# A decoder step: q's norm folded into the output norm, k's norm from rounded parts, and another order of the products in a chunk

## The reference

```python
def l2_normalize(x):
    return x * rsqrt(sum(x * x, axis=-1) + EPS)

q = repeat(l2_normalize(q) * 128 ** -0.5, 2)      # 16 heads of q and k, 32 of v
k = repeat(l2_normalize(k), 2)
decay = where(incl, exp(where(incl, gc_i - gc_j, 0)), 0)
a_mat = where(strict, (k * beta) @ k.T * decay, 0)     # inverted, chunk by chunk
intra = (q @ k.T) * decay
o, S = gated_delta(...)                            # o is linear in q
o = rms_norm(o, gnorm) * silu(z)                   # o * rsqrt(mean(o * o) + EPS) * gnorm
```

## Time and profile before

| what | us |
|---|---|
| median of 3 executions | 2893.99 (2893.37 to 2894.33) |
| profiled execution, its own time | 2895.47 |
| its span, first to last instruction | 2893.6 |
| TensorE busy | 2870.3 (99%) |
| VectorE busy | 1795.9 (62%) |
| ScalarE busy | 1418.8 (49%) |
| GpSimd busy | 193.8 (7%) |

### The profile page before, as it was taken

How to read it: one execution, slowest core, us unless ns; L and a number is a source line. 1 busy time by engine, 2 the same in 40 slices (tenths; PEclk the granted TensorE clock), 3 DMA queues, 4 the chain that set the end, 5 groups by cost and what they waited for, 6 DMA issues and landing times.

```text
span 2893.6 us, 68883 instructions
## 1 busy us (share of the span) xinstructions
PE 2870.3 (99%) x25543; PEld 2794.9 (97%) x25543; DVE 1795.9 (62%) x2868; ACT 1418.8 (49%) x2139; POOL 193.8 (7%) x301
## 2 busy tenths in 40 slices
PE   8999999999999999999999999999999999999999
PEld 7999999999999999999999999999999999999999
DVE  6778788788886455555555444577555555554444
ACT  6656566566564444444444344566444444444343
POOL 0212222122220000000000000000000000000000
PEclk9999999999999999999999999999999999999999
DMA  7666656656555556555555555744455555555554
GB/s 217 181 183 182 192 169 181 192 159 191 170 177 191 192 186 182 178 178 180 181 178 180 180 182 178 219 152 132 168 177 181 181 179 178 180 181 180 178 181 147
DMA packets 521090, 518.97 MB, mean 179 GB/s; under 512 B 32127, under 2 KB 444200, under 8 KB 520664
## 3 DMA queue, kind: packets, MB, share of 16 engines
q1 hardware_dynamic: 519150, 510.34, 56.9%
q0 software_dynamic: 1152, 5.58, 0.6%
q10 hardware_dynamic: 594, 0.25, 0.0%
HBM read 492.12 MB, written 32.82 MB: 181 GB/s over the span
## 4 chain that ended last, share of the span: by engine, by line
PE 67%; DVE 1%; ACT 1%; issue 0%; DMA 0%; DVEq 0%; ACTq 0%
PE bank L484 11%; PE bank L486 11%; PE bank L485 11%; PE upper L486 11%; PE upper L484 11%; PE upper L485 11%; PE upper L1013 0%; ACT w_hi L465 0%; PE upper L1037 0%; PE upper L1025 0%; DMA x_res<-x_spill 0%; DVE w_lo L472 0%; PE upper L1014 0%; PE upper L1150 0%; ACT scores L798 0%
## 5 line engine op out<-in xcount | busy, mean ns | idle before, releaser
L472 DVE TENSOR_TENSOR w_lo<-w_raw,w_hi 128x1024 fp32r<-128x1024 f32 x858 | 1049.7, 1223 | 933.5 <-ACT w_hi L465 929.0
L465 ACT ACTIVATE w_hi<-w_raw 128x1024 fp32r<-128x1024 f32 x858 | 908.8, 1059 | 1263.5 <-PE bank L486 736.0
L484 PE MATMUL bank<-h_hi,w_hi 128*128 128x264 f32 x3168 | 937.1, 296 | 3.4 <-DVE w_lo L472 3.4
L485 PE MATMUL bank<-h_lo,w_hi 128*128 128x264 f32 x3168 | 901.1, 284 | 0.0
L486 PE MATMUL bank<-h_hi,w_lo 128*128 128x264 f32 x3168 | 900.4, 284 | 0.0
L484 PEld LDWEIGHTS bank<-h_hi,w_hi 128*128 128x128 f32 x3168 | 598.0, 189 | 24.6 <-issue 12.1
L485 PEld LDWEIGHTS bank<-h_lo,w_hi 128*128 128x128 f32 x3168 | 598.8, 189 | 1.3
L486 PEld LDWEIGHTS bank<-h_hi,w_lo 128*128 128x128 f32 x3168 | 597.3, 189 | 0.0
L484 PE MATMUL upper<-h_hi,w_hi 128*128 128x264 f32 x1456 | 415.3, 285 | 0.0
L486 PE MATMUL upper<-h_hi,w_lo 128*128 128x264 f32 x1456 | 414.2, 284 | 0.0
L485 PE MATMUL upper<-h_lo,w_hi 128*128 128x264 f32 x1456 | 413.5, 284 | 0.0
(11 more groups left out here) (429 smaller groups left out, 4057.3 us busy)
## 6 DMA issues: line engine op xcount, KB each, us to landing
w_raw<-in_w_gate_up_dram SPq DMA_DIRECT2D x704, 256.0 KB, 2.9
w_raw<-in_w_in_a_dram SPq DMA_DIRECT2D x388, 256.0 KB, 3.2
w_raw<-in_w_down_dram SPq DMA_DIRECT2D x352, 256.0 KB, 2.9
w_raw<-in_w_out_a_dram SPq DMA_DIRECT2D x128, 256.0 KB, 3.1
s_dec<-in_state_delta_dram SPq DMA_DIRECT2D x32, 512.0 KB, 5.7
out_dram<-s_dec SPq DMA_DIRECT2D x32, 512.0 KB, 5.0
w_raw<-in_w_q_b_dram SPq DMA_DIRECT2D x64, 256.0 KB, 3.2
w_raw<-in_w_o_b_dram SPq DMA_DIRECT2D x64, 256.0 KB, 2.9
```

The costliest lines, as they stand in the source:

```text
L465: nc.scalar.activation(w_hi[:, s % SPL, :], w_raw[:, s, :], ACT.Copy).then_inc(hi_ready, 1)
L472: ops.tensor_tensor(w_lo[:, s % SPL, :], w_raw[:, s, :], w_hi[:, s % SPL, :].bitcast(F32), ALU.subtract).then_inc(lo_ready, 1)
L484: nc.tensor.matmul(bank[bk][:, 0:T], wh, xh, start=first, stop=False)
L485: nc.tensor.matmul(bank[bk][:, 0:T], wh, xl, start=False, stop=False)
```

## The change

Four edits.

1. q is not normalised. Its squares, scaled by `P * EPS ** 0.5`, are kept (`q_sq`, ScalarE, n = 13 of the next turn) and added by VectorE to the squares of both heads' outputs at n = 21, ahead of the decode updates (`on_added`). The output's norm has another constant. Step 23 waits for `on_added`. q's Ln, Exp and product go.
2. k's sum of squares is made of two fp32r products: ScalarE rounds the squares (`k_hl[:, 0]`), VectorE takes the rest (`k_hl[:, 1]`, n = 19), and `early` waits for both.
3. The causal mask moves into the exponent: `ET` is the minimum of the difference and `floor`, 0 or -1e30. `masked_decay` on GpSimd goes.
4. `tiles` waits for `hi_ready`, makes the two products with the high part for its tiles, and the low products of all 8 tiles come last, after `lo_ready`. With two calls, the first has 4 tiles' high products (8), the second the other 8 and then 8 low ones.

```diff
         def tiles(pe, c, tl, part=None, ends=None):
...
             if part in (None, 0):
+                pe.wait_ge(hi_ready, 4 * q + (s + 1))
+            for t, bk, xh, xl, first, last in tl if part is None else tl[4 * part:4 * part + 4]:
+                nc.tensor.matmul(bank[bk][:, 0:T], high(t), xh, start=first, stop=False)
+                nc.tensor.matmul(bank[bk][:, 0:T], high(t), xl, start=False, stop=False)
+            if part in (None, 1):
                 pe.wait_ge(lo_ready, 4 * q + (s + 1))
-            for n, (t, bk, xh, xl, first, last) in enumerate(tl):
...
-                nc.tensor.matmul(bank[bk][:, 0:T], wh, xh, start=first, stop=False)
-                nc.tensor.matmul(bank[bk][:, 0:T], wh, xl, start=False, stop=False)
-                m = nc.tensor.matmul(bank[bk][:, 0:T], wl, xh, start=False, stop=last)
+                for t, bk, xh, xl, first, last in tl:
+                    m = nc.tensor.matmul(bank[bk][:, 0:T], low(t), xh, start=False, stop=last)
                 m.then_inc(w_used, 1)
...
-            def masked_decay(g):
...
-                pool.tensor_tensor(intraT[:, :, :], ET[:, :, :], bc(incl, 1, 4), ALU.mult).then_inc(incl_ready, 1)
...
+            nc.scalar.activation(ones_r[:, :], ones, ACT.Copy).then_inc(aux_copied, 1)
+            nc.scalar.activation(floor[:, :], incl, ACT.Copy, bias=MASKED, scale=-MASKED).then_inc(aux_copied, 1)
...
-                nc.scalar.activation(qk_sq[:, :, :], qk[:, :, :], ACT.Square).then_inc(sq_ready, 1)
+                nc.scalar.activation(k_sq[:, :], qk[:, 1, :], ACT.Square).then_inc(sq_ready, 1)
+                act.wait_ge(sq_ready, 3 * g + 1)
+                nc.scalar.activation(k_hl[:, 0, :], k_sq[:, :], ACT.Copy).then_inc(sq_ready, 1)
...
+                elif n == 13:
+                    after(act, on_added, G)
+                    nc.scalar.activation(q_sq[:, :], qk[:, 0, :], ACT.Square, scale=float(P * EPS ** 0.5)).then_inc(q_sq_ready, 1)
...
                     pe.wait_ge(on_sq, G + 1)
-                    pe.wait_ge(rn_ln, 2 * min(G + 1, GROUPS - 1) + 2)
+                    pe.wait_ge(rn_ln, min(G + 1, GROUPS - 1) + 1)
+                    pe.wait_ge(on_added, G + 1)
...
-                pe.wait_ge(sq_ready, g + 1)
+                pe.wait_ge(sq_ready, 3 * g + 3)
...
-                for i in range(2):
-                    m = nc.tensor.matmul(B[i][:, 0:T], ones, qk_sq[:, i, :], start=True, stop=True)
-                m.then_inc(ss_ready, 1)
+                nc.tensor.matmul(B[0][:, 0:T], ones_r[:, :], k_hl[:, 0, :], start=True, stop=False)
+                nc.tensor.matmul(B[0][:, 0:T], ones_r[:, :], k_hl[:, 1, :], start=False, stop=True
+                                 ).then_inc(ss_ready, 1)
...
-                    tiles(pe, c, tl[0:4], 0)
+                    tiles(pe, c, tl, 0)
...
-                    tiles(pe, c, tl[4:8], 1)
+                    tiles(pe, c, tl, 1)
...
-                    ts(ET[:, m_, :], gcb[:, h, c * P:(c + 1) * P], sc_g[:, m_:m_ + 1], 0.0, ALU.subtract,
-                       ALU.min).then_inc(et_pre, 1)
+                    stt(ET[:, m_, :], gcb[:, h, c * P:(c + 1) * P], sc_g[:, m_:m_ + 1], floor[:, :], ALU.subtract,
+                        ALU.min).then_inc(et_pre, 1)
+                elif n == 19:
+                    dve.wait_ge(sq_ready, 3 * g + 2)
+                    tt(k_hl[:, 1, :], k_sq[:, :], k_hl[:, 0, :].bitcast(F32), ALU.subtract).then_inc(sq_ready, 1)
                 elif n == 23:
...
-                    tt(qk[:, :, :], qk[:, :, :], qk_sq[:, :, :], ALU.mult).then_inc(qn_ready, 1)
+                    tt(qk[:, 1, :], qk[:, 1, :], k_sq[:, :], ALU.mult).then_inc(qn_ready, 1)
...
-                    dve.wait_ge(incl_ready, G + 1)
-                    tt(hc(intraT[:, :, :]), pairs(0), hc(intraT[:, :, :]), ALU.mult
-                       ).then_inc(intra_ready, 1)
+                    tt(hc(intraT[:, :, :]), pairs(0), hc(ET[:, :, :]), ALU.mult).then_inc(intra_ready, 1)
...
                 elif n in (21, 22, 23):
+                    if n == 21:
+                        dve.wait_ge(on_sq, G + 1)
+                        dve.wait_ge(q_sq_ready, G + 1)
+                        tt(sqn[:, :, :], sqn[:, :, :], bc(q_sq[:, :], 1, 2), ALU.add).then_inc(on_added, 1)
```

More of the change, by code:

```diff
@@ L351, in yoco_step @@
         sq_ready = sem("sq_ready")
+        q_sq_ready = sem("q_sq_ready")
+        on_added = sem("on_added")
         ss_ready = sem("ss_ready")
@@ L478, in tiles @@
             q, s = c
-            if part in (None, 0):
-                pe.wait_ge(lo_ready, 4 * q + (s + 1))
-            for n, (t, bk, xh, xl, first, last) in enumerate(tl):
-                wh = w_hi[:, s % SPL, t * P:(t + 1) * P]
-                wl = w_lo[:, s % SPL, t * P:(t + 1) * P]
-                nc.tensor.matmul(bank[bk][:, 0:T], wh, xh, start=first, stop=False)
-                nc.tensor.matmul(bank[bk][:, 0:T], wh, xl, start=False, stop=False)
-                m = nc.tensor.matmul(bank[bk][:, 0:T], wl, xh, start=False, stop=last)
-                if ends is not None and last and n < len(tl) - 1:
-                    m.then_inc(ends, 1)
-            if part in (None, 1):
+            high = lambda t: w_hi[:, s % SPL, t * P:(t + 1) * P]
+            low = lambda t: w_lo[:, s % SPL, t * P:(t + 1) * P]
+            if ends is not None:
+                pe.wait_ge(lo_ready, 4 * q + (s + 1))
+                for n, (t, bk, xh, xl, first, last) in enumerate(tl):
+                    nc.tensor.matmul(bank[bk][:, 0:T], high(t), xh, start=first, stop=False)
+                    nc.tensor.matmul(bank[bk][:, 0:T], high(t), xl, start=False, stop=False)
+                    m = nc.tensor.matmul(bank[bk][:, 0:T], low(t), xh, start=False, stop=last)
+                    if last and n < len(tl) - 1:
+                        m.then_inc(ends, 1)
+                m.then_inc(w_used, 1)
+                return
+            if part in (None, 0):
+                pe.wait_ge(hi_ready, 4 * q + (s + 1))
+            for t, bk, xh, xl, first, last in tl if part is None else tl[4 * part:4 * part + 4]:
+                nc.tensor.matmul(bank[bk][:, 0:T], high(t), xh, start=first, stop=False)
+                nc.tensor.matmul(bank[bk][:, 0:T], high(t), xl, start=False, stop=False)
+            if part in (None, 1):
+                pe.wait_ge(lo_ready, 4 * q + (s + 1))
+                for t, bk, xh, xl, first, last in tl:
+                    m = nc.tensor.matmul(bank[bk][:, 0:T], low(t), xh, start=False, stop=last)
                 m.then_inc(w_used, 1)
-            return m
         def load(sp, c, *halves):
@@ L2460, in first_turn @@
                     else:
-                        for n in (10, 11, 12, 13, 23):
+                        for n in (10, 11, 12, 13, 19, 23):
                             early(0, n)
```

35 lines of the change are left out of this document (17 added, 18 removed).

## The result

The changed kernel takes 2905.39 us (median of 6 runs, 2904.79 to 2906.60) against 2894.79 us of the kernel before (6 runs on the same chip, 2893.37 to 2896.25): 10.6 us or 0.38% slower, ratio 1.0038, 95% interval 1.0026 to 1.0050.

A forecast was written before the change was run, and what follows sets the result against it. TensorE's own instructions bound the kernel. 14 steady turns +14.0, turn 1 +0.5, last turn +1.1, start -1.9, L484's wait -0.5, attention +1.0 give +14.2 us, 2908.2 us; own range 2902 to 2914, stated range 2889 to 2918.

The forecast's parts named there:

- Step 5: Delta-rule turn: TensorE comes 0.49 us sooner after the even step than VectorE's input allows; 0.27 us late.
- step 15: Delta-rule turn: TensorE comes sooner than ScalarE's input allows; 0.27 us late.
- step 19: Delta-rule turn, last part of this step: TensorE comes sooner than VectorE's input allows; 0.35 us late.
- step 22: Delta-rule turn: TensorE waits for the fourth decode update, behind VectorE's added q squares; 0.74 us late, between 0.6 and 0.9.
- the sums: `early` sums of squares in each turn: 0.88 us before, 0.25 as two fp32r products; 0.63 us saved.
- The 0.14 behind a producer: Extra cost from a producer's end to the first product behind a waiting step, read in the last turn; 0.14 us.
- The tap: VectorE's convolution tap beside the masked decay: 1.52 us becomes 0.49, so 1.03 us come back before step 22's chain.
- The start: Before the first `early` and behind it: waiting for the high part alone gains about 2.1 us, 1.9 after two new copies.
- I take 0 and keep both ends: Fp32r products with new neighbours cost 0.121 us as before; 0.5 ns either way would make 10 us.
- The rival at 2898: All chunks: the new order has its own price, 0.5 ns less per product, 10 us below the forecast; chance 0.06.
- The attention: Last heads of the attention: two odd steps have no room, 0.5 us each, +1.0 us.
- The inputs are there: Rival: odd steps and step 22 together wait under 0.63 us, only the sums' saving counts; 12 us faster, 2882; chance 0.12.

The follow-up runs named there:

- a_half_late: Kernel before plus edits 1 to 3, addition behind the decode updates, two-call chunks 8 high then 4 low products per call, one-call low last: 2880.86 us, ratio 0.9952.
- a_half: Kernel before plus edits 1 to 3, addition ahead of the updates, two-call chunks 8 high then 4 low products per call, one-call low last: 2889.93 us, ratio 0.9982.
- b_order: Kernel before with edit 4 alone (low products of a chunk last, wait for the high part only): 2923.13 us, ratio 1.0095.
- b_mask_order: Kernel before with edits 3 and 4 (mask inside the exponent, new order of products), q and k as before: 2911.01 us, ratio 1.0049.
- b_one: Kernel before with the new order of products only in chunks taken in one call (feed-forward, projections): 2888.65 us, ratio 0.9978.

## Why the prediction was right, and where it was off

The forecast was +14.2 us (2908.2); the spans give +11.2 and the medians +10.6, inside its own range of 2902 to 2914. That the steady turn came out is no luck: its waits were found at the places and nearly in the sizes named, but for two errors of 0.1 us that cancel. That the total is only 3.0 us off is partly luck: the start lost 2.0 us more than forecast, and the feed-forward stages, the attention and the end gave 5.5 that were not. One of the two signs that the prediction named as proving it wrong came true: the turn is right and the feed-forward stages have changed. The terms, by the landmarks of both traces (starts of the `early` sums and of the sums of squares in the norms):

| term | forecast | measured |
|---|---|---|
| 14 steady turns | +14.0 | +14.4 |
| start and turn 1 | -1.4 | +0.6 |
| last turn and to the first norm behind it | +0.6 | +0.7 |
| first feed-forward stage | 0 | -2.1 |
| k and v projection and attention | +1.0 | +0.4 |
| second feed-forward stage | 0 | -2.1 |
| the end | 0 | -0.7 |
| sum | +14.2 | +11.2 |

- **A steady turn**, +1.00 forecast, +1.03 measured. Step 5 0.27 (measured 0.23), step 15 0.27 (0.29), step 19 0.35 (0.37), step 22 0.74 (0.63), the sums -0.63 (measured -0.53). The sums and the wait of step 22 were both put 0.1 too large, and these errors cancel. The 1.13 us in the earlier trace rows hold two sums and the outer product behind them, which the prediction took as 0.25:

```profile
592.40 0.58 PE L1909 MATMUL upper<-dec_dr,kmask 96*128 96x256 f32 x2
```

  From its start to the tiles at 592.82 it takes 0.42 us. So the sums took 0.71; as two fp32r products they take 0.26 (a_half_late), 0.45 less, and the outer product is 0.08 shorter. The 0.14 behind a producer, used four times, is mostly the same slip: 905.23 + 4 x 0.27 + 0.07 is 906.38 and not 906.35, and of the 0.36 us from there to 906.74 the outer product takes 0.34 and not 0.25. In the kernel after, 0.02 to 0.11 us lie between a producer's end and the step that waits for it. The mechanisms are shown one by one: a_half against after for the distances, a_half against a_half_late for the addition.
- **The tap.** The forecast needed VectorE to be 1.03 us sooner because the masked decay goes. The tap takes 0.48 us now (by forms, busy us and mean ns of one, of the kernel after):

```profile
L2252 DVE SCALAR_TENSOR_TENSOR cacc<-craw,convw,cacc 128x264 f32<-128x264 f32 x64 | 30.4, 496 | 0.0
...
L2271 DVE SCALAR_TENSOR_TENSOR ET<-gcb,sc_g,floor 128x128 f32<-128x128 f32 x64 | 20.6, 344 | 0.0
```

  The rule of the Trainium skill (SBUF — State Buffer, section "SBUF: two separate sides") that a VectorE instruction with two SBUF inputs and a GpSimd one that reads SBUF exclude each other agrees with this and with b_order's `dec_sel`, 1.70 us beside 0.61. The forecast used it for the tap alone, and thus did not see that the mask edit is also what saves step 19, 12 us of a time that would else be about 2917 (an estimate, from b_order and b_mask_order).
- **The masks** were put at about 0.28 us each; with three operands they take 0.344. Nothing waits for it in a steady turn.
- **The start.** The step that failed is "the start gains: ... which leaves 1.9". The masks and k's low part were seen as the next thing late, with the sums at 70.95; they came at 71.32, 0.26 of it by the masks, which took 1.12 us together instead of 0.86. TensorE came there at 69.18 and not at 69.0 (1.22 and 0.76 make 1.98, not the 2.2 of the sum), which costs nothing, since it stands. Then the clock was at half, which cost 1.5 us. At step 4 the kernel after was thus 0.1 us ahead (81.51 against 81.62) instead of 1.9, and from there to the second sums it lost 0.7 at steps 5, 15 and 19, where 0.5 was forecast. That a stand of TensorE can cost more than its length was not in the sum.
- **The order's own price.** The step "I take 0 and keep both ends" was mis-sized: the order is cheaper, by 4.2 us in the two feed-forward stages; in the first it is 2.13 us over some 6350 products (772.81 / 0.1217), 0.34 ns each. The rival at 2898 had the sign and, with 0.5 ns on all products, the order of size; the runs show it only where a chunk is taken in one go, and the start went the other way.
- **The attention**, +1.0 forecast, +0.4 measured. The waits view lists one of the two waits (L1050 <- f_sq, 0.5 us), and by b_one the order takes 0.3 us off this stretch; where the rest lies is not shown.
- **"The inputs are there"** needed steps 5, 15, 19 and 22 to wait less than 0.63 us together. They wait 1.5.
- The forecast expected waits at L1894, L2008 and L2062 in the waits view. They are there in the distances, but only the first is listed.

## What to carry to other kernels

When a full engine's own instructions are put in another order, set the end of each input against the new start: the same products with 12 between the steps instead of 8 made 0.94 us a turn of difference, 15.5 us in all (a_half against the changed kernel). Ask of each edit what it covers for the others: a wait that is taken away uncovers the next one (step 22, then 23), and an edit that gives nothing alone (the mask) can be worth 12 us beside another. And look for waits in the distances between landmarks of the two traces too, since two of 0.29 and 0.37 us here were missing from the waits view.

## What the runs showed of the hardware

- Fp32r products of 128x128 by 128x264 are cheaper with the low ones of 8 tiles together at the end: 772.81 against 770.68 us for the same stage, 0.28%. In groups of 4 tiles, inside the turn, nothing was seen (52.29 us either way). The cause is open.
- A 2.14 us stand of TensorE, two sums and eight products, and another stand of 0.5 us were followed by some 4 us at half clock (0.58 granted), and four products of 1.13 us took 2.08. One stand of 2.15 us was followed by the same in b_mask_order (0.57 from 74 to 78 us), and one of 2.14 in b_order was not (1.00).
- VectorE's pair of 128x8 operations, 0.61 us, took 1.70 us beside one GpSimd multiplication of 128x512.
